# FFN matmuls on x * (1 + scale), with the RMS factor and the shift applied to their result

## The chip, the cores and the metric

One NeuronCore of a Trainium2 chip runs the whole program. The metric is the device time of one execution, in microseconds: the median of several runs.

## The reference, cut to what matters

The program is one inference step of a small diffusion backbone with 128 context tokens and 512 latent tokens of 1024 channels. Four layers have the mixers Fourier, pooling, latent attention and Fourier again; each mixer is followed by a gated ConvFFN (2816 gate and 2816 value channels). Context and latent tokens have shifts, scales and gates of their own, and are separate sequences for the convolution.

```
def modulate(x, shift, scale):
    return rms_norm(x) * (1 + scale) + shift          # rms_norm: x * rsqrt(mean(x*x) + eps), per token
def dwconv3(u, w, b):                                   # zeros beside the first and the last token
    up = jnp.pad(u, ((0, 0), (1, 1), (0, 0)))
    return up[:, :-2] * w[0] + up[:, 1:-1] * w[1] + up[:, 2:] * w[2] + b
def conv_ffn(h, w_in, w_conv, b_conv, w_out):
    u = dwconv3(h @ w_in, w_conv, b_conv)
    gate, val = jnp.split(u, 2, axis=-1)
    return (jax.nn.silu(gate) * val) @ w_out
...
    sh1, sc1, g1, sh2, sc2, g2 = split(silu(cond) @ w_ada[i] + b_ada[i], 6)
    x = x + g1 * mixer(modulate(x, sh1, sc1))
    x = x + g2 * conv_ffn(modulate(x, sh2, sc2), w_ffn_in[i], ...)
```

## The kernel before

Activations lie with channels on the 128 partitions: `x` is 8 chunks of 128 channels by W = 644 token columns, context in columns 0 to 127, latent in 130 to 641, gaps between and behind. A matrix product is made of three fp32r products: every operand is split into a rounded part (`_hi`) and the remainder (`_lo`), and hi*hi, hi*lo and lo*hi are summed. One result (128 output channels by all tokens) takes 8 chunks x 3 products x 2 halves of 322 columns = 48 matmuls into one of two PSUM accumulators, `acc[0]` and `acc[1]`, in turn. TensorE (PE) may start result j + 2 only when result j has been taken out of its accumulator (`result_taken`).

The weights come as one stream of units of 512 KB, in a fixed order (`_stream`), through four slots `raw`: SyncE (SP) loads the next unit of a slot once the slot's last unit is done (`unit_done`). A weight unit is rounded by ScalarE (ACT, L790) as soon as the result two places ahead is ready, and its remainder is taken by GpSimd (POOL, L344), which frees the slot. A modulation unit is 128 rows of `w_ada`: VectorE (DVE) multiplies it by the two conditions, with a running sum (`modulate`, L1261, two products of 128x1024), which frees its slot. The 48 modulation units of the next layer are computed in this layer's FFN.

A mixer ends in a projection of eight results. DVE adds each, times its gate, to a chunk of `x` (`update_x`, L1239, three pieces), ACT squares the chunk (L840), and DVE adds the squares (L1248). In layer 0 the projection also computes eight modulation units, in steps of `PRODUCT_STEPS`. In the pooling layer a projection result takes only 12 matmuls.

The FFN begins with `norm`: PE sums the squares over channels with a matmul by ones (`statistics`, L462), ACT takes the root (L804), DVE the reciprocal (L1154); then for every chunk DVE scales (L1163) and modulates (L1185), ACT rounds (L832), POOL takes the remainder (L354). PE's `first_two` takes the chunks of the first two results as they come.

FFN-in and FFN-out go in three parts of 8, 8 and 6 pairs (`PARTS`). A pair is a gate result and a value result. For each, ACT rounds the next weight, then writes the centre tap and bias (L887, L893), and DVE adds the left and right taps (L1307, L1311), which frees the accumulator. ACT takes the silu of the gate (L890), DVE multiplies by the value (L1317), ACT rounds (L896), DVE takes the remainder (L1321). In the layers before the last, DVE computes one modulation unit ahead of each pair and one after the gate's taps. A part ends in eight FFN-out results of 8, 8 or 6 chunks, each added to `x`; part 1 has four more modulation units there.

Of the kernel before, what the change touches and what calls it, by code (L numbers as in the profile page):

```python
# [28 lines left out]
GAP = 2  # L29
LAT0 = CTX + GAP  # L30
LAT1 = LAT0 + LAT
W = LAT1 + GAP
# [16 lines left out]
KW = KEYS + GAP  # L49
# [22 lines left out]
Q_TILES = [(LAT0 + P * t, LAT0, SHALF, 2) for t in range(4)] + [(0, 0, CTX, 1)]  # L72
# [11 lines left out]
def ada_in_ffn(layer):  # L84

    return layer + 1 < DEPTH

ADA_EXTRA, EXTRA_PART = MODS - 2 * PAIRS, 1  # L90

FIRST_MODS, PRODUCT_MODS = 2 * KC, KC
# [17 lines left out]
def extra(layer, part):  # L112
    return ADA_EXTRA if ada_in_ffn(layer) and part == EXTRA_PART else 0


class Counts:


    def __init__(self):
        self.unit = 0  # L120
        self.result = 0
        self.split = 0
        self.ada = 0
        self.pair = 0
        self.rounded = 0
        self.stat = 0
        self.chunk = 0
        self.full = 0
        self.affine = 0
        self.squared = 0  # L130
        self.score = 0
        self.cleared = 0
# [8 lines left out]
def build_backbone(nc, a):  # L141
# [8 lines left out]
    with ExitStack() as ctx:  # L150
# [30 lines left out]
        gate_pool = place("gate_pool", [P, KC, 2])  # L181
        top, negtop, total, inverse = (place(n, [P, 2]) for n in ("top", "negtop", "total", "inverse"))
# [43 lines left out]
        sum_q, rstd_q = row(3), row(4)  # L226
        probs = [row(3), row(4)]
# [37 lines left out]
        h_ready = sem("h_ready")  # L265
        mod_ready = sem("mod_ready")
# [23 lines left out]
        CXS, LTS = slice(0, CTX), slice(LAT0, LAT1)  # L290
# [21 lines left out]
        def after_ffn_in(n, layer, count):  # L312
            n.unit += 4 * count if ada_in_ffn(layer) else 2 * count
            n.split += 2 * count
            n.result += 2 * count
            n.pair += count
            n.ada += 2 * count if ada_in_ffn(layer) else 0

        def after_project(n, units=KC, squares=True):
            n.unit += units  # L320
            n.split += units
            n.result += KC
            n.squared += KC if squares else 0
# [15 lines left out]
        def _(pool):  # L339
# [43 lines left out]
            def project(size, last=False):  # L383

                for j in range(6 if last else 8):
                    ring((j + 2) % SLOTS, n.split + 2 + j, size if j < 6 else UNIT)

            def ffn(layer):
                lo_parts()
                n.stat += 1  # L390
                for part, (_, count) in enumerate(PARTS):
                    if ada_in_ffn(layer):
                        with pool.Fori(0, count) as i:
                            ring(0, n.split + 2 * i + 2)
                            ring(1, n.split + 2 * i + 3)
                    else:
                        with pool.Fori(0, count // 2) as i:
                            for j in range(4):
                                ring((j + 2) % SLOTS, n.split + 4 * i + 2 + j)
                    after_ffn_in(n, layer, count)  # L400
                    project(count * P, part == 2 and layer == DEPTH - 1)
                    after_project(n, squares=part == 2)
# [33 lines left out]
        def _(pe):  # L436
# [80 lines left out]
            def ffn(layer):  # L517
                norm()
                for part, (_, count) in enumerate(PARTS):
                    turn = 1 if ada_in_ffn(layer) else 2  # L520

                    def gate_or_value(i, j):
                        pe.wait_ge(unit_done[j], n.unit // SLOTS + i + 1)
                        pe.wait_ge(result_taken, n.result + 2 * turn * i + j - 1)
                        for k in range(KC):
                            done = product(acc_halves(j % 2), weights(j, k),
                                           token_halves(h_hi[:, k, :], h_lo[:, k, :]), k == 0, k == KC - 1)
                        done.then_inc(result_ready, 1)

                    if part == 0:  # L530

                        first_two()
                        for j in range(2, 2 * turn):
                            gate_or_value(0, j)
                    with pe.Fori(int(part == 0), count // turn) as i:
                        for j in range(2 * turn):
                            gate_or_value(i, j)
                    after_ffn_in(n, layer, count)
                    project((g_hi, g_lo), count, g_ready, n.pair - count, (extra(layer, part), 0))
                    after_project(n, squares=part == 2)  # L540

            def fnet(layer):
                r = n.result
                for g in range(GROUPS):
                    for t in range(5):

                        first = 0 if t == 0 else LAT0 + P * (t - 1)
# [95 lines left out]
            def attention():  # L643
                with pe.Fori(0, 2) as i:
                    for h2 in range(2):
# [22 lines left out]
                        def values(t):  # L668

                            p = accumulator(V_RESULT + t)  # L670
                            first = [0, LAT0, LAT0 + P, LAT0 + 2 * P, LAT0 + 3 * P, LAT1][t]
# [111 lines left out]
        def _(act):  # L783
# [24 lines left out]
            def norm(layer, shift, scale, mine=lambda c: False, target=None, after_root=None, after_chunk=None):  # L808
# [4 lines left out]
                for c in range(KC):  # L813
                    out = row(HF + c % 2) if target is None else padded[c % 2]
                    if mine(c):
                        act.wait_ge(xn_ready, n.chunk + c + 1)
# [20 lines left out]
                n.chunk += KC  # L837

# [3 lines left out]
            def project_steps(i, squares, rounds=4):  # L842

                for j in range(4):
                    if j < rounds:
                        round_ring((j + 2) % SLOTS, n.unit // SLOTS + i + (j + 2) // SLOTS + 1, n.result + 4 * i + j + 1)
                    if squares:
# [921 lines left out]
```

## Time and profile before

| what | us |
|---|---|
| median of 3 runs | 3133.83 |
| lowest and highest run | 3130.42, 3135.1 |
| span of the profiled execution, first to last instruction | 3126.8 |
| median less that span | 7.0 |
| PE busy / DVE busy / POOL busy in the span | 2755.8 / 1636.7 / 946.0 |

The busy times are sums over the span, and engines work side by side, so they don't add up to it. The profile gives no time of its own for the profiled execution beside its span; the runs are timed separately.

### The profile page before, as it was taken

The page shows a single profiled execution, that of the slowest core. Times are in us where ns is not written, and L with a number is a line of the kernel's source. Part 1 is how long each engine was busy: PE and PEld are TensorE (multiplying, and loading weights), DVE is VectorE, ACT ScalarE, POOL GpSimd, SP SyncE. Part 2 cuts the span into 40 slices and gives each one's busy share as a digit, 9 for nine tenths or more (in the row PEclk, how much of TensorE's full clock was granted, in tenths as well). Part 3 has the DMA queues.
Part 4 walks back from the last instruction along what each step waited for, and adds up shares of the span by engine and source line. Part 5 has one row for each costly group of instructions (what it writes and reads, how often), then busy time and mean ns, then how long its engine had stood idle before and what let it go on. Part 6 is the DMA issues. An engine that isn't in the chain of part 4 may idle for free.

```text
span 3126.8 us, 46036 instructions
## 1 busy us (share of the span) xinstructions
PE 2755.8 (88%) x17344; PEld 2663.9 (85%) x17344; DVE 1636.7 (52%) x2448; ACT 919.5 (29%) x1247; POOL 946.0 (30%) x420
## 2 busy tenths in 40 slices
PE   3887999997399999978898987999999697999997
PEld 3676999996299999977887886999999487999997
DVE  7667636465875574654433335736655525323235
ACT  3112323233232232332322223323223322323232
POOL 2014333333543333332110113333333213333332
PEclk9998999998699999989988888999999898999999
DMA  7332424343033343321110111424433101222221
GB/s 254 101 121 95 145 92 144 127 138 105 27 115 121 114 149 113 132 71 65 41 41 28 36 46 40 154 101 135 146 116 121 62 21 50 72 74 74 74 74 68
DMA packets 83942, 297.48 MB, mean 95 GB/s; under 512 B 10048, under 2 KB 11520, under 8 KB 83456
## 3 DMA queue, kind: packets, MB, share of 16 engines
q1 hardware_dynamic: 78336, 285.25, 27.2%
q10 hardware_dynamic: 5504, 10.79, 1.0%
q8 instruction: 74, 1.21, 0.2%
q14 instruction: 28, 0.23, 0.0%
HBM read 293.07 MB, written 2.93 MB: 95 GB/s over the span
## 4 chain that ended last, share of the span: by engine, by line
PE 78%; DVE 13%; ACT 3%; issue 3%; DMA 1%; POOL 1%; ACTq 0%; DVEq 0%; SPq 0%; POOLq 0%
PE acc L443 75%; DVE rows L1185 2%; DVE rows L1163 2%; PE sacc L443 2%; DVE rows L1154 1%; DMA raw<-in_stream 1%; DVE products L1261 1%; DVE rows L1248 1%; DVE pt_lo L1206 1%; PE sacc L462 1%; PE acc L700 1%; POOL w_lo L344 0%; DVE scratch L1405 0%; DVE x L1239 0%; POOL h_lo L354 0%
## 5 line engine op out<-in xcount | busy, mean ns | idle before, releaser
L344 POOL TENSOR_TENSOR w_lo<-raw,w_hi 128x1024 fp32r<-128x1024 f32 (+2 forms) x336 | 815.7, 2428 | 2021.1 <-ACT w_hi L790 2021.1
L443 PE MATMUL acc<-h_hi,w_hi 128*128 128x322 f32 x3408 | 802.9, 317 | 152.4 <-POOL h_lo L354 76.1
L443 PE MATMUL acc<-h_lo,w_hi 128*128 128x322 f32 x3408 | 798.1, 316 | 0.0
L443 PE MATMUL acc<-h_hi,w_lo 128*128 128x322 f32 x3408 | 792.1, 314 | 0.0
L443 PEld LDWEIGHTS acc<-h_hi,w_hi 128*128 128x128 f32 x3408 | 583.6, 192 | 171.4 <-issue 113.3
L790 ACT ACTIVATE w_hi<-raw 128x1024 fp32r<-128x1024 f32 (+2 forms) x336 | 350.2, 1043 | 1060.6 <-PE acc L443 1008.3
L443 PEld LDWEIGHTS acc<-h_lo,w_hi 128*128 128x128 f32 x3408 | 587.9, 193 | 0.0
L443 PEld LDWEIGHTS acc<-h_hi,w_lo 128*128 128x128 f32 x3408 | 587.8, 193 | 0.0
L1261 DVE SCALAR_TENSOR_TENSOR products<-raw,cond 128x1024 f32<-128x1024 f32 x372 | 474.2, 1315 | 18.3 <-ACT cond L1101 8.6
L1239 DVE SCALAR_TENSOR_TENSOR x<-acc,mod,x 128x128 f32 (+1 forms) x360 | 136.4, 434 | 453.3 <-PE acc L443 453.3
L1307 DVE SCALAR_TENSOR_TENSOR conv<-acc,conv_w,conv 128x644 f32<-128x644 f32 x176 | 156.6, 890 | 399.3 <-ACT conv L893 292.7
L443 PE MATMUL acc<-g_hi,w_hi 128*128 128x322 f32 x1408 | 328.1, 314 | 18.7 <-DVE g_lo L1321 13.2
L443 PE MATMUL acc<-g_lo,w_hi 128*128 128x322 f32 x1408 | 326.9, 313 | 0.0
L443 PE MATMUL acc<-g_hi,w_lo 128*128 128x322 f32 x1408 | 326.6, 313 | 0.0
L443 PEld LDWEIGHTS acc<-g_hi,w_hi 128*128 128x128 f32 x1408 | 241.3, 191 | 22.7 <-DVE g_lo L1321 16.5
L443 PEld LDWEIGHTS acc<-g_lo,w_hi 128*128 128x128 f32 x1408 | 240.9, 191 | 0.0
L443 PEld LDWEIGHTS acc<-g_hi,w_lo 128*128 128x128 f32 x1408 | 240.6, 190 | 0.0
L1248 DVE TENSOR_TENSOR rows<-rows 128x644 f32<-128x644 f32 x82 | 122.3, 1491 | 120.7 <-ACT rows L840 62.1
L1311 DVE SCALAR_TENSOR_TENSOR conv<-acc,conv_w,conv 128x644 f32<-128x644 f32 x176 | 156.6, 890 | 27.7 <-DVE conv L1307 27.0
L896 ACT ACTIVATE g_hi<-gated 128x644 f32 x88 | 65.4, 743 | 273.3 <-DVE gated L1317 273.3
L890 ACT ACTIVATE gated<-conv 128x644 f32<-128x644 f32 x88 | 65.8, 748 | 190.1 <-DVE conv L1311 190.1
L1321 DVE TENSOR_TENSOR g_lo<-gated,g_hi 128x644 f32 x88 | 73.1, 831 | 91.5 <-ACT g_hi L896 91.5
(155 smaller groups left out, 2540.7 us busy)
## 6 DMA issues: line engine op xcount, KB each, us to landing
raw<-in_stream SPq DMA_DIRECT2D x544, 512.0 KB, 3.3
x<-in_x ACTq DMA_DIRECT2D x8, 322.0 KB, 10.2
out_y<-y ACTq DMA_DIRECT2D x8, 322.0 KB, 3.0
cond<-in_cond ACTq DMA_DIRECT2D x2, 1024.0 KB, 6.3
inv_count<-in_inv_count ACTq DMA_DIRECT2D x1, 1328.0 KB, 6.3
rows<-in_rope ACTq DMA_DIRECT2D x1, 644.0 KB, 4.7
conv_w<-in_conv_w ACTq DMA_DIRECT2D x4, 88.0 KB, 2.0
cache<-in_cache ACTq DMA_DIRECT2D x1, 320.0 KB, 2.9
```

Source lines behind the costliest of these rows:

```text
L344: nc.gpsimd.tensor_tensor(lo, raw[slot][:, 0:raw_size], hi.bitcast(f32), ALU.subtract).then_inc(unit_done[slot], 1)
L443: done = nc.tensor.matmul(o, lhs[lp], r, start=first and z == 0, stop=last and z == 2)
L790: nc.scalar.activation(hi, raw[slot][:, 0:size], ACT.Copy).then_inc(weights_hi, 1)
L890: nc.scalar.activation(gated[:], conv[0][:, 1:W + 1], ACT.Silu).then_inc(silu_done, 1)
L896: nc.scalar.activation(g_hi[:, ds(gate, 1), :].rearrange("p o t -> p (o t)"), gated[:], ACT.Copy).then_inc(g_rounded, 1)
L1163: nc.vector.tensor_tensor(row(XN[c % 3]), x[:, c, :], row(RSTD), ALU.mult).then_inc(xn_ready, 1)
L1239: done = nc.vector.scalar_tensor_tensor(xs, acc[pair][:, bank, p0:p0 + x1 - x0], gate(cond_), xs, ALU.mult, ALU.add)
L1248: nc.vector.tensor_tensor(total_, total_, row(SQ), ALU.add).then_inc(inc, 1)
L1261: nc.vector.scalar_tensor_tensor(out[z][:], raw[slot][:], 1.0, cond[:, z, :], ALU.mult, ALU.mult, accum_out=mod[:, layer % 2, ds(index, 1) ...
L1307: nc.vector.scalar_tensor_tensor(to, halves(acc[half]), tap(0), to, ALU.mult, ALU.add).then_inc(left_done, 1)
L1311: nc.vector.scalar_tensor_tensor(to, halves(acc[half]), tap(2), to, ALU.mult, ALU.add).then_inc(result_taken, 1)
L1321: nc.vector.tensor_tensor(g_lo[:, gc, :].rearrange("p o t -> p (o t)"), gated[:], g_hi[:, gc, :].rearrange("p o t -> p (o t)").bitcast(f32 ...
```

## The change

RMSNorm's factor is one number per token, so it commutes with the product over channels. The FFN now multiplies `x * (1 + scale)`, split into `g_hi` and `g_lo` chunk by chunk in the mixer's projection (`scaled_hi` on ACT, `scaled_lo` on DVE). The shift, negated, is put into the gap columns, so that the product with the weights comes out there too (`gaps_hi`, `gaps_lo`): columns 0 and 643 and the two between the sequences. `x` starts at column 1, and the latent tokens at 131.

Each FFN-in result is then multiplied in PSUM, by DVE, by the tokens' RMS factor (`token_rstd`, 1 in the gaps). With minus the shift's product beside the first and last token, and the shift's product times the sum of the three taps added afterwards (`minus_taps`, `shift_out`), the convolution's zero padding comes out as in the reference. That sum and the convolution's bias go into the silu's bias for the gate, and into the multiplication for the value, which is now two instructions (context and latent).

PE's statistics stand within the first FFN result, after chunk 3 (`STATS_AFTER`). Root and reciprocal follow, and the first rescale waits for them. POOL takes no remainders of the FFN's input any more. The results of a part go through `h_hi` and `h_lo` instead of `g_hi` and `g_lo`.

The modulation units: one per pair, after the gate's rescale and ahead of its taps, and 13 in the FFN-out of parts 0 and 1 each (`ADA_AFTER_OUT`). The FFN's loops over pairs and results are written out.

```
+ADA_AFTER_OUT = (2, 2, 2, 2, 2, 1, 1, 1)
...
+def ada_after(layer, kind, part, i):
+    if layer + 1 == DEPTH:
+        return 0
+    if kind == "in":
+        return 1 - i % 2
+    return ADA_AFTER_OUT[i] if part < 2 else 0
...
+def ffn_stream(layer):
+    weights = ffn_weights()
+    order, at, ada_at = [], [], []
+    for n, w in enumerate(weights):
+        at.append(len(order))
+        order.append(w)
+        for _ in range(ada_after(layer, *weights[n - 2]) if n >= 2 else 0):
+            ada_at.append(len(order))
+            order.append(("ada", 0, len(ada_at) - 1))
+    return order, at + [len(order), len(order) + 1], ada_at
...
# PE, ffn
+                    if kind == "in":
+                        if j == 0:
+                            pe.wait_ge(gaps_ready, layer + 1)
                         for k in range(KC):
+                            if j == 0:
+                                pe.wait_ge(h_ready, n.chunk - KC + k + 1)
                             done = product(acc_halves(j % 2), weights(j, k),
+                                           token_halves(g_hi[:, k, :], g_lo[:, k, :]), k == 0, k == KC - 1)
+                            if j == 0 and k == STATS_AFTER:
+                                pe.wait_ge(summed, n.squared)
+                                statistics(row(SUM))
...
# ACT, a mixer's projection
+            def scaled_hi(layer, c):
+                chunk = lambda t, cols: t[:, ds(c, 1), cols].rearrange("p o t -> p (o t)")
+                for z, cols in enumerate((CXS, LTS)):
+                    done = nc.scalar.activation(chunk(g_hi, cols), chunk(x, cols), ACT.Copy,
+                                                scale=mod[:, layer % 2, ds(SC2 + c, 1), z:z + 1
+                                                          ].rearrange("p o t -> p (o t)"))
+                done.then_inc(h_rounded, 1)
...
# ACT, ffn
+                    if kind == "in":
+                        pair, half = i // 2, i % 2
+                        act.wait_ge(rescaled, 2 * (n.pair + pair) + half + 1)
+                        nc.scalar.activation(two(conv[half][:, 1:W + 1]), halves(acc[half]), ACT.Copy,
+                                             scale=conv_w[:, pair + half * PAIRS, 1:2]).then_inc(centered, 1)
+                        if half == 0:
+                            act.wait_ge(result_taken, n.result + j + 1)
+                            for z, cols in enumerate((CXS, LTS)):
+                                done = nc.scalar.activation(gated[:, cols], conv[0][:, cols.start + 1:cols.stop + 1],
+                                                            ACT.Silu, bias=shift_out[:, 0, z:z + 1])
+                            done.then_inc(silu_done, 1)
...
# DVE, a mixer's projection
+            def scaled_lo(layer, c):
+                dve.wait_ge(h_rounded, n.chunk + c + 1)
+                part = lambda t, cols: t[:, ds(c, 1), cols].rearrange("p o t -> p (o t)")
+                for z, cols in enumerate((CXS, LTS)):
+                    done = nc.vector.scalar_tensor_tensor(part(g_lo, cols), part(x, cols), mod_gate(layer, SC2)(c)(z),
+                                                          part(g_hi, cols).bitcast(f32), ALU.mult, ALU.subtract)
+                done.then_inc(h_ready, 1)
...
# DVE, ffn
-                norm(layer, SH2, SC2)
+                dve.wait_ge(rooted, n.stat + 1)
+                for cols in (CXS, LTS):
+                    done = nc.vector.reciprocal(token_rstd[:, cols], row(RSTD)[:, cols])
...
+                    if kind == "out":
...
+                        dve.wait_ge(result_ready, n.result + j + 1)
+                        update_acc(i, mod_gate(layer, G2)(i), j % 2)
+                        if part == 2:
+                            sum_square(n.squared + i)
+                        units(after)
+                        continue
...
+                    dve.wait_ge(result_ready, n.result + j + 1)
+                    nc.vector.tensor_tensor(halves(acc[half]), halves(acc[half]), two(token_rstd), ALU.mult
+                                            ).then_inc(rescaled, 1)
+                    units(after)
+                    dve.wait_ge(centered, k + 1)
+                    nc.vector.tensor_scalar(shift_out[:, half, :], acc[half][:, 0, C1:LAT0],
+                                            minus_taps[:, channel:channel + 1], tap(3), ALU.mult, ALU.add)
+                    to = two(conv[half][:, 2:W + 2])
+                    nc.vector.scalar_tensor_tensor(to, halves(acc[half]), tap(0), to, ALU.mult, ALU.add
+                                                   ).then_inc(left_done, 1)
+                    dve.wait_ge(left_done, k + 1)
+                    to = two(conv[half][:, 0:W])
+                    nc.vector.scalar_tensor_tensor(to, halves(acc[half]), tap(2), to, ALU.mult, ALU.add
+                                                   ).then_inc(result_taken, 1)
+                    if half == 0:
+                        continue
...
+                    for z, cols in enumerate((CXS, LTS)):
+                        done = nc.vector.scalar_tensor_tensor(
+                            gated[:, cols], conv[1][:, cols.start + 1:cols.stop + 1], shift_out[:, 1, z:z + 1],
+                            gated[:, cols], ALU.add, ALU.mult)
+                    done.then_inc(gated_done, 1)
```

## Rows read from the trace of the kernel before

**Rows 1.** The page's busy times, share of the span and instructions of each engine.
```profile
PE 2755.8 (88%) x17344; PEld 2663.9 (85%) x17344; DVE 1636.7 (52%) x2448; ACT 919.5 (29%) x1247; POOL 946.0 (30%) x420
```

**Rows 2.** Busy time by stretch: us and count by engine, granted clock, DMA.
```profile
184.00:250.44 66.44, 60.42 (x384) 59.62 (x384) 46.28 (x71) 12.41 (x14) 18.18 (x7) 0.95 0.34 115
250.44:287.78 37.34, 17.20 (x64) 14.42 (x65) 31.57 (x39) 9.67 (x12) 16.03 (x9) 0.68 0.17 64
288.00:393.70 105.70, 105.70 (x710) 105.70 (x710) 73.95 (x106) 38.71 (x46) 39.80 (x15) 1.00 0.42 144
841.21:876.10 34.89, 15.39 (x65) 12.36 (x65) 29.93 (x38) 8.82 (x12) 16.03 (x9) 0.71 0.05 16
1912.31:1956.22 43.91, 21.74 (x100) 18.30 (x101) 33.23 (x41) 14.85 (x17) 17.46 (x10) 0.73 0.06 16
2604.48:2639.37 34.89, 15.61 (x64) 12.56 (x64) 26.87 (x34) 9.79 (x12) 15.06 (x9) 0.71 0.05 15
```

**Rows 3.** Chain of waits, layer 3, mixer's end to FFN: start us, us, what.
```profile
2599.99 4.49 PE acc L443 x30
...
2606.01 0.75 ACT rows L840
...
2606.79 1.89 DVE rows L1248
...
2608.72 2.53 PE sacc L462 x4
...
2612.16 4.19 DVE rows L1154
```

**Rows 4.** Timeline of one gate result in FFN-in: start us, us, engine, instruction.
```profile
633.67 1.06 ACT L790 ACTIVATE w_hi<-raw 128x1024 fp32r<-128x1024 f32 x1 [6.11 <-PE acc L443]
634.64 0.88 ACT L887 ACTIVATE conv<-acc,conv_w 128x644 f32<-128x644 f32 x1
...
634.81 2.40 POOL L344 TENSOR_TENSOR w_lo<-raw,w_hi 128x1024 fp32r<-128x1024 f32 x1 [3.78 <-ACT w_hi L790]
...
635.67 0.89 DVE L1307 SCALAR_TENSOR_TENSOR conv<-acc,conv_w,conv 128x644 f32<-128x644 f32 x1 [3.54 <-ACT conv L887]
636.72 0.89 DVE L1311 SCALAR_TENSOR_TENSOR conv<-acc,conv_w,conv 128x644 f32<-128x644 f32 x1 [0.16 <-DVE conv L1307]
```

**Rows 5.** Timeline where a unit meets POOL; spread of the unit's line (min/median/max ns).
```profile
627.56 1.22 DVE L1261 SCALAR_TENSOR_TENSOR products<-raw,cond 128x1024 f32<-128x1024 f32 x1
...
628.70 3.42 DVE L1261 SCALAR_TENSOR_TENSOR products<-raw,cond 128x1024 f32<-128x1024 f32 x1
...
627.64 3.39 POOL L344 TENSOR_TENSOR w_lo<-raw,w_hi 128x1024 fp32r<-128x1024 f32 x1 [4.78 <-ACT w_hi L790]
...
L1261 DVE SCALAR_TENSOR_TENSOR products<-raw,cond x372: 1211/1221/3435, 14.2 to 2373.4; 128x1024 f32<-128x1024 f32 x186
```

**Rows 6.** Groups by line (busy us, mean ns), and one line's spread (min/median/max ns).
```profile
L1321 DVE TENSOR_TENSOR g_lo<-gated,g_hi 128x644 f32 x88 | 73.1, 831 | 91.5 <-ACT g_hi L896 91.5
...
L1278 DVE TENSOR_SCALAR mod<-mod 128x16 f32<-128x16 f32 x8 | 1.1, 172 | 0.2
...
L823 ACT ACTIVATE rows<-rows,mod x16: 477/647/802, 59.7 to 2453.5; 128x128 f32<-128x128 f32 x8, 128x512 f32<-128x512 f32 x8
```

**Rows 7.** Timeline of ACT in layer 0's projection: a weight that came late.
```profile
229.49 1.06 ACT L790 ACTIVATE w_hi<-raw 128x1024 fp32r<-128x1024 f32 x1 [12.41 <-DMA raw<-in_stream]
```

**Rows 8.** Timeline of DVE in the pool layer: first and last residual update.
```profile
820.99 1.13 DVE L1239 SCALAR_TENSOR_TENSOR x<-acc,gate_pool,x 128x128 f32<-128x128 f32 x3
...
841.21 1.13 DVE L1239 SCALAR_TENSOR_TENSOR x<-acc,gate_pool,x 128x128 f32<-128x128 f32 x3
```

**Rows 9.** Waits of PE in layer 0's FFN: us in total, times, longest.
```profile
PE acc L443 <- DVE g_lo L1321: 3.3, 3, 2.3
PE acc L443 <- POOL w_lo L344: 1.8, 1, 1.8
```

**Rows 10.** Timeline of PE in the attention: a wait without a cause in the trace.
```profile
1668.08 1.00 PE L443 MATMUL acc<-ckv_hi,w_hi 128*128 128x386 f32 x2 [3.54 <-issue]
```

More of the change, by code:

```diff
@@ L70 @@
 V_RESULT = 4
-Q_TILES = [(LAT0 + P * t, LAT0, SHALF, 2) for t in range(4)] + [(0, 0, CTX, 1)]
+Q_TILES = [(LAT0 + P * t, LAT0, SHALF, 2) for t in range(4)] + [(C0, C0, CTX, 1)]
 FIRST_LOADS = 16 * 3
@@ L309, in head_out, with after_project @@
             return dst[:, ds(4 * i + 2 * h2 + hh, 1), q0:q0 + P].rearrange("p o t -> p (o t)")
[L312 to L319, printed above, removed]
+        def after_project(n, units=KC):
             n.unit += units
@@ L322, in after_project, with after_ffn @@
             n.result += KC
-            n.squared += KC if squares else 0
+            n.squared += KC
+        def after_ffn(n, layer):
+            order, at, ada_at = ffn_stream(layer)
+            n.unit += len(order)
+            n.split += len(at) - 2
+            n.result += len(at) - 2
+            n.pair += PAIRS
+            n.ada += len(ada_at)
+            n.squared += KC
         @block.sync
@@ L517, in ffn @@
             def ffn(layer):
[L518 to L524, printed above, removed]
+                n.chunk += KC
+                _, at, _ = ffn_stream(layer)
+                for j, (kind, part, i) in enumerate(ffn_weights()):
+                    unit = n.unit + at[j]
+                    first, count = PARTS[part]
+                    pe.wait_ge(unit_done[unit % SLOTS], unit // SLOTS + 1)
+                    pe.wait_ge(result_taken, n.result + j - 1)
+                    if kind == "in":
+                        if j == 0:
+                            pe.wait_ge(gaps_ready, layer + 1)
@@ L535, in ffn @@
[L535 to L540, printed above, removed]
+                                           token_halves(g_hi[:, k, :], g_lo[:, k, :]), k == 0, k == KC - 1)
+                            if j == 0 and k == STATS_AFTER:
+                                pe.wait_ge(summed, n.squared)
+                                statistics(row(SUM))
+                    else:
+                        for k in range(count):
+                            if i == 0:
+                                pe.wait_ge(g_ready, n.pair + first + k + 1)
+                            done = product(acc_halves(j % 2), weights(j, k),
+                                           token_halves(h_hi[:, k, :], h_lo[:, k, :]), k == 0, k == count - 1)
@@ L542, in fnet @@
+                    done.then_inc(result_ready, 1)
+                after_ffn(n, layer)
             def fnet(layer):
@@ L906, in fnet @@
+                after_ffn(n, layer)
             def fnet(layer):
@@ L961, in pool_mix @@
                     square(x[:, j, :])
+                    scaled_hi(layer, j)
+                n.chunk += KC
                 after_project(n, 4)
@@ L1224, in unit @@
                     n.ada += 1
-                for _ in range(before):
-                    unit()
+                gaps_lo(layer)
                 for j in range(KC):
-                    update_x(j, j, gate(j), j % 2, squares)
+                    update_x(j, j, gate(j), j % 2, True)
+                    scaled_lo(layer, j)
                     for _ in range(steps[j]):
```

310 lines of the change are left out of this document (156 added, 154 removed).

## The prediction

> **What bounds the kernel now.** The page comes first: TensorE (PE) is busy for 88% of the span, VectorE (DVE) for about half, and GpSimd (POOL) for a third [rows 1]. Then the busy time by stretch, to see where PE is not busy [rows 2]. In the FFN stretch it runs 710 matmuls in 105.7 us, 0.149 us each, with no gap: 48 matmuls, one result, take 7.16 us, and the gate and value results of a pair 14.3 us. There the hardware loops cost nothing, and neither do the modulation units (two per pair, four products on DVE). The four other stretches of [rows 2] run from the end of the mixer's last result to the moment when PE is steady again in the FFN (in the pool layer from the start of the last residual update). In 37.34, 34.89, 43.91 and 34.89 us, PE does 60, 60, 96 and 60 matmuls beside the 4 of the statistics. Less 0.149 us for each, 28.4, 26.0, 29.6 and 26.0 us are lost, 110 us together. The chain of waits shows by what, for layer 3 [rows 3]: update, square (0.75), adding the square (1.89), the statistics (2.53 on PE), root, reciprocal (4.19), and after that scaling, modulation, rounding and remainder chunk by chunk until 2639.37. The granted clock of these stretches is 0.68 to 0.73 [rows 2], between the levels of 1.2 and 2.4 GHz; the loss includes that.
>
> **What the change takes away.** The FFN input no longer waits for the norm. Chunks 0 to 3 of the first result can run as soon as the mixer's last result is out (call it E): 24 x 0.149 = 3.6 us. Then the statistics, which start at E + 4.24 and end at E + 6.77 as now [rows 3]; the remainder of chunk 7 is ready by then (square's sum at E + 4.2, plus two subtractions of about 1.0 us together, by the 0.831 of [rows 6]). Chunks 4 to 7 follow. So 6.77 - 3.6 = 3.2 us are lost instead of 26 to 30.
>
> The root and reciprocal now run beside chunks 4 to 7. Root to E + 7.6, the reciprocal of 640 columns 4.2 [rows 3], fills, tap sums, then the first rescale at about E + 13.2, while result 0 is ready at E + 10.4. It has until E + 17.5, when result 1 is ready and PE wants the buffer back. With rescale, one unit and two taps it is free at about E + 18.6: 1.1 us late, some 0.25 us over the stall below, for three layers 0.75 us.
>
> **What it adds in the mixers.** Per chunk, two ScalarE (ACT) multiplications by (1 + scale) and two DVE remainders. The nearest ACT row has two pointer operands, 0.48 to 0.80 us [rows 6]; a plain rounding would be less, so 0.9 to 1.28 us, 1.1 taken. In the projections of layers 2 and 3 this hides behind 7.16 us of PE per result. In the pool layer nothing hides it, since a chunk there is a serial chain: update, square, sum. Seven chunks take 841.21 - 820.99 = 20.2 us [rows 8], 2.89 each. With the new work update 1.13, square 0.7, ACT 1.1, remainder 1.0 and handovers give 4.1: 8.5 us more, and 2.0 lost after the last update. In layer 0 the projection already loses 66.44 - 57.2 = 9.2 us [rows 2], because its units and weights share four slots and ACT waits for a weight [rows 7]. DVE gets 1 us more per result, of which I carry 2.0 us to the end, plus 0.4 before the statistics. The starts then cost 5.6 + 10.5 + 3.2 + 3.2 + 0.75 = 23 us, and the gain is 110 - 23 = **87 us**.
>
> **What it adds in the FFN.** Now the gate result of a pair, from its readiness T [rows 4]: ACT rounds the next weight, POOL starts its 2.40 us subtraction at T + 1.19, ACT scales the centre, and DVE adds the taps (0.89 + 0.15 + 0.89); PE gets the buffer at T + 4.1 and needs it at T + 7.16. A unit comes after this. In the new order DVE first rescales in PSUM, then computes a unit, then the taps. No row has DVE writing PSUM: between 0.83 (the SBUF remainder, [rows 6]) and twice 0.89; 0.89 taken, and either is covered by POOL's turn.
>
> The unit is the point. A product alone takes 1.21 us, but its longest is 3.435 [rows 5]. At 627.56 a product starts, POOL 0.08 us behind it; POOL takes 3.39 instead of 2.40, and the second product, due at 628.70, ends at 632.12, 1.09 after POOL. They don't run together, and POOL gets the next turn; the taps, which read PSUM, keep their 0.89 beside it [rows 4]. In the new order the unit meets POOL's subtraction in every pair. If POOL is first, it ends at T + 3.58 and the products at T + 5.82; if the first product is first, POOL ends at T + 4.4 and the unit at T + 5.5. DVE is done with the preceding pair only some 0.5 us after T (the silu, the second rounding and the value half are pushed back with the taps), so POOL is first. Then the shift's bias (0.17 to 0.27 us, by the 16-column row of [rows 6] and a pointer more), and taps of 1.93: PE restarts at T + 8.0, **0.85 us late**. Bounds: 0 if unit and POOL did not collide, 0.5 if the product is first, 1.2 if each small step costs 0.1 more. The value half has time to spare. 22 pairs in 3 layers: 66 x 0.85 = **56 us**. Layer 3 has no units, and its gate buffer is free by T + 4.4.
>
> The Trainium skill, "SBUF — State Buffer", section "SBUF: two separate sides", says that a DVE operation with two SBUF inputs and a GpSimd one lock the shared ports for a whole instruction. The trace agrees (3.42 us for 1.22); by it the rescale, with one input in PSUM, and the taps go free. By the rule the FFN stalls as I take it, without it not at all.
>
> From FFN-in to FFN-out the last remainder of a part now lags the stalls: PE idles 1.6, 1.6 and 3.4 us at the three parts, against 3.3 + 1.8 now [rows 9] (the 1.8, a weight behind four units, goes). That is 1.5 a layer in three layers and 0.25 per part in layer 3: **5 us**.
>
> The units moved to FFN-out: five results of eight in two parts get two. POOL again goes first, so DVE ends them at T + 8.1, 1 us into the next result, where the update fits beside POOL. PE needs only the update, done at T + 2.1. Slots: the next units' loads can start at T + 3.6 and T + 5.8, the next weight's at T + 8.1; with 3.5 us each the weight lands near T + 11.6 and is rounded at T + 14.3. Cost nothing, with 2.7 us of cover. Unrolled loops: nothing. One wait at the head of a long loop's second pass shows 3.54 us without a cause [rows 10]; straight-line stretches before it show none.
>
> **Sum**, on the profiled span of 3126.8: -87 + 56 + 5 = -26, hence 3101. The median of the runs, 3133.8, lies 7.0 above that span, which I carry: **3108 us**.
>
> **Rivals.**
> A, unit and POOL do not collide (the unit gets through before POOL, or ACT's rounding is late). For it: 1.221 is the median product [rows 5]. Against: POOL starts 1.14 after ACT in [rows 4]. Then the 56 goes: 3133.8 - 87 + 5 = 3052.
> B, slower: the four slots stall PE in FFN-out. For it: three loads of 512 KB per result, and layer 0's projection loses 9.2 us over eight results with eight units. Against: there the weights stand ahead of the units, here they alternate, with 2.7 us to spare. At 9.2 us in each of six stages 55 us: 3163. It decides from 26 / 6 = 4.3 us a stage.
> C, the starts are shortened less: the first rescale waits for root, reciprocal, fills and taps. Each us beyond E + 13.2 costs one us in each layer; at 6 us the gain is gone: 3132.
>
> **How the numbers follow.** Forecast 0.60, A 0.17, B 0.10, C 0.13. The forecast's own range, by 0.5 to 1.1 us of stall, is 3085 to 3125. The range, 3054 to 3136, takes in A's end and C's, and leaves B and the tails out. 0.2% is 6 us, about what the runs' spread of 4.7 us can tell. Faster: nearly all of the forecast (0.57), A, and 0.06 of C: 0.80. The same: 0.03 and 0.05: 0.08. Slower: B and 0.02: 0.12.
>
> **What would show it.** Right: at the four starts a PE gap of 1 us before the statistics, no lowered clock, h_lo of POOL gone. In the FFN of layers 0 to 2 a pair of 15.1 us, the second product at 3.4 or the first delayed; in layer 3 14.3. Pairs of 14.3 everywhere show A; PE waiting for w_lo in FFN-out shows B; a first rescale later than E + 14 shows C. I am wrong if a stall stands where I have none, above all in layer 3.

## The result, and the profile after

The changed kernel takes 3059.5 us (median of 4 runs, 3056.5 to 3062.1) against 3132.1 us of the kernel before on the same chip (4 runs, 3129.3 to 3135.1): ratio 0.9773, 95% interval 0.9758 to 0.9789, or 73 us less. I had forecast 3108. The direction and the range held; the change is nearly three times the 26 us of my sum. The profiled execution took 3058.1 us with a span of 3056.2, so the two profiled spans differ by 70.6 us.

The page's busy times, the line that answers to [rows 1]: DVE is busy 337 us longer, POOL 40 us less. Not all of the 337 is work: a product that waits for POOL counts as busy, and the same 372 products take 189 us more (their row on the page before, L1261, and on the page after, L1330). The new rescales are 147 us.

```profile
PE 2737.8 (90%) x17344; PEld 2641.5 (86%) x17344; DVE 1973.7 (65%) x2900; ACT 919.0 (30%) x1375; POOL 905.9 (30%) x388
...
L1261 DVE SCALAR_TENSOR_TENSOR products<-raw,cond 128x1024 f32<-128x1024 f32 x372 | 474.2, 1315 | 18.3 <-ACT cond L1101 8.6
L1330 DVE SCALAR_TENSOR_TENSOR products<-raw,cond 128x1024 f32<-128x1024 f32 x372 | 663.3, 1828 | 9.3 <-ACT cond L1143 8.1
```

Busy time by stretch (columns as in [rows 2]): the four starts, from the mixer's last result (pool layer: from the start of the last residual update) to steady work of PE, and 105.7 us of layer 0's FFN.

```profile
252.34:273.04 20.70, 17.14 (x101) 16.32 (x100) 17.62 (x34) 8.07 (x12) 4.74 (x2) 0.92 0.47 161
836.24:853.76 17.52, 14.78 (x84) 13.84 (x83) 14.68 (x30) 5.70 (x8) 4.74 (x2) 0.90 0.23 72
1878.41:1897.12 18.71, 15.61 (x100) 14.78 (x100) 15.82 (x30) 9.85 (x11) 4.91 (x2) 1.00 0.21 67
2557.40:2574.70 17.30, 15.60 (x100) 14.77 (x100) 13.52 (x26) 6.76 (x9) 4.80 (x2) 1.00 0.18 62
288.00:393.70 105.70, 103.17 (x684) 101.50 (x684) 83.40 (x111) 36.04 (x49) 38.53 (x15) 1.00 0.34 107
```

When PE is steady, two whole results (96 matmuls, 14.3 us) are done. So the starts lose 6.4, 3.2, 4.4 and 3.0 us. Layer 0's last projection result comes 1.9 us later than before (252.34 for 250.44), and the pool layer's chunk takes 3.81 us instead of 2.89, 6.4 us over seven. With these the losses are 8.3, 9.6, 4.4 and 3.0 us, 25 together, where 110 were lost before. The 1.9 us are not shown to come from the change: in three profiles of each kernel (experiment 8), layer 0's statistics start at 256.1, 259.4 and 257.7 us before, and at 258.7, 258.3 and 257.9 after. The granted clock of the last two starts is 1.00, for 0.73 and 0.71 in [rows 2]. The last line shows the price: 684 matmuls where the same length held 710 before (0.96 us of it is a wait at the end of part 0, which falls into this window only after the change).

The chain of waits at layer 3's start (start us, us, what), against [rows 3]: the statistics take 1.37 us instead of 2.53, and root, reciprocal and fills run while PE has the other chunks. PE waits for the first pair's taps until 2574.70, and from there on runs 672 matmuls in 100.11 us, 0.149 each, without a gap: layer 3 has no units and no stall.

```profile
2561.71 1.37 PE sacc L491 x4
...
2563.93 4.17 DVE rows L1353 x2
...
2568.92 1.47 DVE minus_taps L1365
...
2570.85 0.85 DVE acc L1399
...
2574.70 100.11 PE acc L472 x672
```

The timeline of one pair in layer 0's FFN-in, to be read against [rows 4, 5]; the gate result is ready at about T = 280.42, when its last two matmuls (from 279.94) are through.

```profile
279.54 0.83 DVE L1423 TENSOR_TENSOR h_lo<-gated,h_hi 128x644 fp32r<-128x644 f32 x1 [0.81 <-ACT h_hi L936]
280.24 0.46 PE L472 MATMUL acc<-g_hi,w_hi 128*128 128x322 f32 x2
280.44 0.84 DVE L1399 TENSOR_TENSOR acc<-acc,rows 128x644 f32<-128x644 f32 x1
280.50 1.06 ACT L822 ACTIVATE w_hi<-raw 128x1024 fp32r<-128x1024 f32 x1 [0.99 <-PE acc L472]
281.19 1.22 DVE L1330 SCALAR_TENSOR_TENSOR products<-raw,cond 128x1024 f32<-128x1024 f32 x1
281.64 3.01 POOL L377 TENSOR_TENSOR w_lo<-raw,w_hi 128x1024 fp32r<-128x1024 f32 x1 [4.27 <-ACT w_hi L822]
282.33 3.40 DVE L1330 SCALAR_TENSOR_TENSOR products<-raw,cond 128x1024 f32<-128x1024 f32 x1
...
286.77 0.89 DVE L1410 SCALAR_TENSOR_TENSOR conv<-acc,conv_w,conv 128x644 f32<-128x644 f32 x1
287.57 0.83 DVE L1399 TENSOR_TENSOR acc<-acc,rows 128x644 f32<-128x644 f32 x1
287.80 0.53 PE L472 MATMUL acc<-g_hi,w_hi 128*128 128x322 f32 x2 [0.27 <-DVE conv L1410]
...
295.21 0.84 DVE L1399 TENSOR_TENSOR acc<-acc,rows 128x644 f32<-128x644 f32 x1
```

The unit does meet POOL: its second product takes 3.40 us and POOL 3.01. But DVE is done with the preceding pair at 280.37, 0.05 us ahead of T, so the first product starts 0.45 us ahead of POOL. The taps end at T + 7.24. PE began the value result at 280.24, could begin the next gate result 7.16 us later, at 287.40, and begins it at 287.80. The next rescale of a gate comes 14.77 us after the last (280.44 to 295.21), 0.47 over the 14.30 of a pair of layer 3, which has no stall (seven pairs in the 100.11 us above).

PE's waits in layer 2's FFN (us in total, times, longest), against [rows 9]: taps and remainders, no weight.

```profile
PE acc L472 <- DVE conv L1410: 7.2, 19, 2.4
PE acc L472 <- DVE h_lo L1423: 4.3, 3, 2.4
```

### The profile page after: what moved, and what is told of

It reads as the page before. It is cut to its first block, busy times and chain, and to the rows that moved or that the text cites. A ratio compares the mean times of both kernels' runs of the same rounds, so it can differ in the third digit from the quotient of the medians.

```text
span 3056.2 us, 43498 instructions
## 1 busy us (share of the span) xinstructions
PE 2737.8 (90%) x17344; PEld 2641.5 (86%) x17344; DVE 1973.7 (65%) x2900; ACT 919.0 (30%) x1375; POOL 905.9 (30%) x388
## 4 chain that ended last, share of the span: by engine, by line
PE 64%; DVE 26%; issue 5%; ACT 4%; DMA 1%; POOL 0%; ACTq 0%; DVEq 0%; SPq 0%; POOLq 0%
PE acc L472 61%; DVE products L1330 11%; DVE conv L1410 2%; DVE conv L1406 2%; PE sacc L472 2%; DVE rows L1317 1%; DVE rows L1205 1%; DVE rows L1196 1%; DVE rows L1227 1%; DVE x L1311 1%; DVE pt_lo L1249 1%; DVE shift_out L1403 1%; DVE rows L1353 1%; ACT w_hi L822 1%; DMA raw<-in_stream 1%
## 5 line engine op out<-in xcount | busy, mean ns | idle before, releaser
L472 PE MATMUL acc<-g_hi,w_hi 128*128 128x322 f32 x2816 | 654.8, 313 | 21.1 <-DVE conv L1410 19.4
L1330 DVE SCALAR_TENSOR_TENSOR products<-raw,cond 128x1024 f32<-128x1024 f32 x372 | 663.3, 1828 | 9.3 <-ACT cond L1143 8.1
L472 PE MATMUL acc<-g_lo,w_hi 128*128 128x322 f32 x2816 | 650.7, 312 | 0.0
L472 PE MATMUL acc<-g_hi,w_lo 128*128 128x322 f32 x2816 | 649.5, 311 | 0.0
L472 PE MATMUL acc<-h_hi,w_hi 128*128 128x322 f32 x2000 | 475.5, 320 | 109.0 <-POOL h_lo L399 51.2
L472 PEld LDWEIGHTS acc<-g_hi,w_lo 128*128 128x128 f32 x2816 | 479.0, 189 | 0.0
L472 PE MATMUL acc<-h_lo,w_hi 128*128 128x322 f32 x2000 | 470.7, 317 | 0.0
L472 PE MATMUL acc<-h_hi,w_lo 128*128 128x322 f32 x2000 | 468.0, 316 | 0.0
L472 PEld LDWEIGHTS acc<-h_hi,w_hi 128*128 128x128 f32 x2000 | 345.4, 194 | 122.4 <-issue 73.8
L472 PEld LDWEIGHTS acc<-h_lo,w_hi 128*128 128x128 f32 x2000 | 347.9, 194 | 0.0
L472 PEld LDWEIGHTS acc<-h_hi,w_lo 128*128 128x128 f32 x2000 | 347.5, 194 | 0.0
```

The lines of the kernel that those rows point to most:

```text
L472: done = nc.tensor.matmul(o, lhs[lp], r, start=first and z == 0, stop=last and z == 2)
L1330: nc.vector.scalar_tensor_tensor(out[z][:], raw[slot][:], 1.0, cond[:, z, :], ALU.mult, ALU.mult, accum_out=mod[:, layer % 2, ds(index, 1) ...
```

## The experiments

Four questions were open: how the unit and POOL stall a pair, whether the order of the two decides the size, what the statistics' speed hangs on, and why layer 2's attention, which the change leaves alone, was 11 us shorter in the profile after. Experiment 4 takes the change apart, 6 and 7 go on from it. In the diffs, minus lines are those of the changed kernel.

**1. The unit behind the taps.**

```
                     nc.vector.tensor_tensor(halves(acc[half]), ...).then_inc(rescaled, 1)
-                    units(after)
                     dve.wait_ge(centered, k + 1)
...
                     ... tap(2) ... .then_inc(result_taken, 1)
+                    units(after)
                     if half == 0:
                         continue
```

> The gate half's unit stands behind the two taps instead of ahead of them. Theory (turns): the 0.45 us that a pair of layers 0 to 2 loses (14.77 against 14.32 in layer 3's pace) is the unit's second product waiting out POOL's subtraction with the taps queued behind it. Then the pair falls to 14.3 and 66 pairs give back about 30 us: 3030 us, with the products at 1.2 us each, since POOL is done by T + 4. Rival (chain): the rescale, the shift's bias and the scaled centre are by themselves too long for the buffer. Then the pair stays near 14.8 and the time at 3059 us.

Measured: 3025.4 us, ratio 0.9667 (0.9644 to 0.9689), 33 us below the changed kernel by the two ratios. DVE's timeline: rescale, products undisturbed, and the next gate's rescale 14.27 us later. PE's waits for remainders fall too, to 3.0 us a layer from 4.4. The rival falls.

```profile
293.61 0.84 DVE L1399 TENSOR_TENSOR acc<-acc,rows 128x644 f32<-128x644 f32 x1 [0.54 <-PE acc L472]
...
297.37 1.22 DVE L1330 SCALAR_TENSOR_TENSOR products<-raw,cond 128x1024 f32<-128x1024 f32 x1
298.51 1.22 DVE L1330 SCALAR_TENSOR_TENSOR products<-raw,cond 128x1024 f32<-128x1024 f32 x1
...
307.88 0.84 DVE L1399 TENSOR_TENSOR acc<-acc,rows 128x644 f32<-128x644 f32 x1 [0.54 <-PE acc L472]
```

**2. The unit where it was, POOL later.** ACT rounds the next weight behind the scaled centre in the gate half.

```
-                    if j + 2 < len(weights) or layer < DEPTH - 1:
-                        round_unit(...)
+                    if not gate and (j + 2 < len(weights) or layer < DEPTH - 1):
+                        ahead()                       # the same round_unit
...
                         nc.scalar.activation(two(conv[half][:, 1:W + 1]), ...).then_inc(centered, 1)
+                        if gate:
+                            ahead()
```

> DVE's order stays; only ACT's rounding of the next weight stands behind the scaled centre in the gate half, so that POOL's subtraction starts some 1.3 us later, at about T + 2.9. Theory (turns): both products run before POOL, the taps end near T + 5.4, and the pair falls to 14.3: 3030 us. Rival (work): it is the unit's 2.4 us of work ahead of the taps that stalls, whatever POOL does: the pair stays at 14.8, 3059 us.

Measured: 3018.8 us, ratio 0.9645 (0.9615 to 0.9675), 40 us below the changed kernel by the ratios; from the first experiment it can't be told. With the unit still ahead of the taps, both products run in 1.22 us, POOL comes just before the second ends, and the pair takes 14.27.

```profile
295.56 0.84 DVE L1405 TENSOR_TENSOR acc<-acc,rows 128x644 f32<-128x644 f32 x1 [0.54 <-PE acc L472]
296.31 1.22 DVE L1336 SCALAR_TENSOR_TENSOR products<-raw,cond 128x1024 f32<-128x1024 f32 x1
297.45 1.22 DVE L1336 SCALAR_TENSOR_TENSOR products<-raw,cond 128x1024 f32<-128x1024 f32 x1
298.26 2.68 POOL L377 TENSOR_TENSOR w_lo<-raw,w_hi 128x1024 fp32r<-128x1024 f32 x1 [6.23 <-ACT w_hi L822]
...
309.83 0.84 DVE L1405 TENSOR_TENSOR acc<-acc,rows 128x644 f32<-128x644 f32 x1 [0.54 <-PE acc L472]
```

So the stall is the meeting, not the unit's work. The Trainium skill, "SBUF — State Buffer", section "SBUF: two separate sides", says that of a DVE operation with two SBUF inputs and a GpSimd one that reads SBUF the one that starts first keeps the shared ports for its whole length; the 3.40 of the changed kernel and the 1.22 here agree with it.

**3. POOL first.** Three operations of two columns, their result unused, delay the unit behind POOL.

```
+                    for d in range(3 * after):
+                        nc.vector.tensor_scalar(spare[:, d, :], minus_taps[:, 0:2], minus_taps[:, 2:3], tap(3),
+                                                ALU.mult, ALU.add)
                     units(after)
```

> Three small DVE operations (about 0.5 us together, their result unused) stand between the gate half's rescale and its unit, so that POOL's subtraction starts ahead of the first product. Theory (turns, the order decides): the unit then ends 0.77 us later than now however long the small operations take between 0.45 and 1.2 us, and the pair goes from 14.77 to about 15.5: +50 us, 3110 us, with a first product of about 3.2 us and two undisturbed ends. Rival (the order does not matter): the pair grows by the small operations alone, 0.5 us: +33 us, 3093.

Measured: 3108.5 us, ratio 0.9919 (0.9893 to 0.9944), 46 us above the changed kernel. The pair takes 15.36 us. One detail was not as expected: the small operations themselves wait out POOL (2.88 us for three that take 0.66 at 276.13, where POOL is idle), and the products behind them run free.

```profile
276.13 0.66 DVE L1403 TENSOR_SCALAR spare<-minus_taps,conv_w 128x2 f32<-128x2 f32 x3
...
289.85 0.46 PE L473 MATMUL acc<-g_hi,w_hi 128*128 128x322 f32 x2
...
290.05 0.83 DVE L1400 TENSOR_TENSOR acc<-acc,rows 128x644 f32<-128x644 f32 x1 [1.59 <-PE acc L473]
290.79 2.88 DVE L1403 TENSOR_SCALAR spare<-minus_taps,conv_w 128x2 f32<-128x2 f32 x3
291.24 2.40 POOL L378 TENSOR_TENSOR w_lo<-raw,w_hi 128x1024 fp32r<-128x1024 f32 x1 [5.82 <-ACT w_hi L823]
293.58 1.21 DVE L1331 SCALAR_TENSOR_TENSOR products<-raw,cond 128x1024 f32<-128x1024 f32 x1
...
298.01 0.54 PE L473 MATMUL acc<-g_hi,w_hi 128*128 128x322 f32 x2 [0.88 <-DVE conv L1414]
...
305.41 0.84 DVE L1400 TENSOR_TENSOR acc<-acc,rows 128x644 f32<-128x644 f32 x1
```

The unit ends at 295.95, 5.9 us after the rescale began, against 5.3 in the changed kernel. The stall is 15.36 - 14.30 = 1.06 us; for POOL first I had forecast 0.85. The value result begins at 289.85, 0.18 us before T as above, so T is 290.03 and PE goes on at T + 7.98 (298.01), where the prediction has T + 8.0; but it could have begun at 289.85 + 7.16, which is T + 6.98 and not T + 7.16. The growth of 0.59 is between the 0.5 and the 0.77 of the two expectations, and the small operations were longer than I took them (0.66 undisturbed, for 0.5), so the size alone decides nothing. The timeline does: POOL takes its turn first, the small operation that stands there waits for its end, and the products behind it no longer stretch.

**4. The units as before, with the new algebra.** Two per pair and four in part 1's FFN-out: the one half of the change alone.

```
     if kind == "in":
-        return 1 - i % 2
-    return ADA_AFTER_OUT[i] if part < 2 else 0
+        return 1
+    return int(part == 1 and i < 4)
```

> The new FFN with the units placed as before: two per pair in FFN-in and four in FFN-out of part 1. Theory (turns): a unit that meets POOL takes 4.5 us of DVE; two of them with two rescales (1.7), two biases (0.5), four taps (3.5), gating (0.75) and remainder (0.8) come to 16.4 us, so DVE becomes the bound of a pair: about 2 us over 14.77, 66 times, 130 us: 3190 us. Rival (only the gate half's buffer is short): one more stall of 0.45 per pair, 3090 us. If the moving of the units did nothing, 3059.

Measured: 3082.7 us, ratio 0.9846 (0.9822 to 0.987), 23 us above the changed kernel: neither number came. POOL does not hold up the second unit, because in the value half ACT rounds the weight behind the silu, and POOL comes when the second product already runs. There it is POOL that waits (3.20 us for 2.40):

```profile
291.39 1.22 DVE L1330 SCALAR_TENSOR_TENSOR products<-raw,cond 128x1024 f32<-128x1024 f32 x1
292.53 1.22 DVE L1330 SCALAR_TENSOR_TENSOR products<-raw,cond 128x1024 f32<-128x1024 f32 x1
292.81 3.20 POOL L377 TENSOR_TENSOR w_lo<-raw,w_hi 128x1024 fp32r<-128x1024 f32 x1 [5.08 <-ACT w_hi L822]
```

DVE then fills the pair (14.86 us, 283.52 to 298.38) and falls behind, so PE waits longer for the last remainder of each part: 7.5 us in layer 0 instead of 4.4. By the ratios the change is worth 71 us: the new algebra with the units as before gives 48 of them (0.9846), and the moving of the units the other 23. Of these 23, PE's waits for taps and remainders in the whole profile show 15 (50.3 us against 35.5); where the others lie is not shown.

**5. The statistics ahead of chunk 0.**

```
+                            if j == 0 and k == 0:
+                                pe.wait_ge(summed, n.squared)
+                                statistics(row(SUM))
                             done = product(...)
-                            if j == 0 and k == STATS_AFTER:
-                                ...
```

> The changed kernel with the statistics ahead of chunk 0 of the first FFN result instead of behind chunk 3, so that PE stands idle for about 4.2 us before them, as it did before. Theory (the statistics took 1.37 us instead of 2.53 because PE was at work until just before them): they take 2.5 us again, and each of the four starts loses 4.2 + 2.5 - 3.6 hidden, less what the wait for the rescale hides: between 1.2 and 5 us a layer, 5 to 20 in all, 3065 to 3080 us. Rival (it is the other code around them): they stay at 1.4 us.

Measured: 3067.9 us, ratio 0.9806 (0.9782 to 0.9829), 10 us above the changed kernel, with intervals that overlap. PE waits 4.3 us for the sum in layer 3, as it did before the change, and the statistics of the four starts take 2.48 to 2.49 us. The chain of layer 2:

```profile
1885.75 2.49 PE sacc L491 x4
```

The windows of the statistics (columns as in [rows 2]) have the clock, here in layer 2 and in the changed kernel in layer 3:

```profile
1885.75:1888.24 2.49, 2.49 (x5) 1.69 (x6) 0.78 (x2) 0.15 (x1) 0.00 (x0) 0.50 0.67 211
2561.71:2563.08 1.37, 1.37 (x6) 1.04 (x7) 0.87 (x2) 0.00 (x0) 0.00 (x0) 1.00 0.59 176
```

So the statistics run in 1.37 us where PE was at work until 0.7 us before (layers 2 and 3, granted clock 1.00, the level of 2.4 GHz), and in 2.49, near twice as long, after 4.3 us of rest or more (granted clock 0.50, the level of 1.2 GHz). Between these it is not fixed: in layer 0 of the changed kernel PE rests 2.75, 3.14 and 3.28 us before them in its three profiles, and they take 1.35, 2.52 and 1.83 us. The rival falls: all four starts went back to 2.5 us, and in layer 0 one and the same code gives three durations.

**6. Shorter head.** The first edit, and the fills and tap sums ahead of the wait for the root.

```
-                dve.wait_ge(rooted, n.stat + 1)
-                for cols in (CXS, LTS): ... reciprocal ...
                 for cols in (slice(0, C0), slice(C1, LAT0), slice(LAT1, W)): ...
                 ... minus_taps ...
+                dve.wait_ge(rooted, n.stat + 1)
+                for cols in (CXS, LTS): ... reciprocal ...
+                clear_sum()
```

> The gate half's unit behind the taps, as in the first experiment, and besides the fills and the two tap sums of the FFN's head ahead of the wait for the root. Theory (the first rescale still comes late in every layer, by the work between reciprocal and rescale): the first rescale comes 1 to 2 us earlier, the 0.8 to 0.95 us that PE waits for the first pair's taps go, and the four layers give back 3 to 5 us: about 3021 us beside 3025. Rival (hidden: PE has the second result to work on meanwhile): no change that can be measured, 3025 us.

Measured: 3013.4 us, ratio 0.9635 (0.961 to 0.9659). The wait is gone from the chain: behind layer 3's statistics PE runs on for 124 matmuls and more.

```profile
2511.34 1.35 PE sacc L491 x4
2512.69 18.42 PE acc L472 x124
```

In time it can't be told from the first edit alone (0.9644 to 0.9689). Its median is the lowest of all versions, 117 us below the kernel before on its chip; the interval of the second experiment overlaps with its own as well.

**7. The way from FFN-in to FFN-out.** The first two results of each part, interleaved on PE, on top of the sixth edit.

```
+                        if i == 0:
+                            pe.wait_ge(unit_done[unit % SLOTS], unit // SLOTS + 1)     # the second result's weight
+                            pe.wait_ge(result_taken, n.result + j)
+                            for k in range(count - 1):
+                                out(j + 1, k)
+                            pe.wait_ge(g_ready, n.pair + first + count)
+                            out(j, count - 1).then_inc(result_ready, 1)
+                            done = out(j + 1, count - 1)
```

> The kernel with early fills, and besides the first two FFN-out results of each part interleaved on PE: all pairs but the last for both, then the last pair's for both. Theory (PE waits at the three transitions of a layer only for the last pair's remainder, 3.0 us per layer with the units out of the way, 4.4 in the changed kernel): the waits go, and the four layers give back 12 us: about 3001 us beside 3013. Rival (the wait moves to the second result's weight or buffer): the waits stay, under another name, 3013 us.

Measured: 3055.5 us, ratio 0.9775 (0.9753 to 0.9796), 42 us slower than the sixth. PE's waits in layer 0's FFN:

```profile
PE acc L472 <- POOL w_lo L377: 9.9, 3, 3.9
```

The remainder's wait is gone, and a worse one stands in its place. By the edit both weight buffers come free at almost the same moment, and the chain at the first transition shows the third result's weight behind it: PE until 383.32, rounding 1.07, POOL 3.28, PE from 388.07. The rival's place was right; its price, none, was not. In the four layers these waits are 35.6 us, where the sixth had 12.0 for remainders, 24 more. Of the other 18 us the two profiles show 13 in layer 2's attention (558.5 and 545.2 us from statistics to statistics), a stretch that differs between executions of one kernel too, as the next experiment shows.

**8. The same kernels again.** For the stretch of layer 2's attention.

> The kernel before once more, unchanged, for the stretch from the start of layer 2's norm statistics to the start of its FFN statistics: 561.8 us in the profile before, 551.0 after, with the same code. Theory (the change sets the pace there, by when the stretch begins): 561.8 again within 2 us. Rival (it differs from execution to execution): another value, anywhere from 548 to 562.

> The changed kernel once more, unchanged, for the same stretch of layer 2. Theory (the change sets the pace there): 551.0 us again within 2 us. Rival (it differs from execution to execution): another value from 548 to 562.

> A third profile of the kernel before, for the stretch of layer 2 from the last chunk of the attention's norm to the FFN's statistics: 531.2 and 525.3 us in the two so far. If the pace there differs from execution to execution and the code around it does not matter, it falls anywhere between 515 and 531; if the kernel before is slower there, between 525 and 531.

> A third profile of the changed kernel, for the same stretch: 520.4 and 528.8 us in the two so far. If the pace differs from execution to execution alone, it falls anywhere between 515 and 531; if the changed kernel is faster there, nearer to 520 than the kernel before.

The first two expectations count from the norm's statistics, the others from the chunk behind that norm with which PE begins; I use the latter, up to the FFN's statistics. The stretch ends with the projection, where the change does add work on ACT and DVE, and after the change it holds the first 24 matmuls of the FFN besides. Counted from the norm's statistics, the three profiles have 561.8, 555.9 and 557.9 us before, and 551.0, 559.4 and 551.0 after: the first theory (the same again within 2 us) fails for both kernels. From the chunk on, the kernel before gives 531.2, 525.3 and 527.3 us, the changed one 520.4, 528.8 and 520.4. Windows of that stretch (columns as in [rows 2]), the second profile of the kernel before:

```profile
1385.92:1911.19 525.27, 462.65 (x2897) 436.57 (x2897) 205.85 (x405) 155.76 (x322) 91.04 (x44) 0.91 0.14 48
```

The first profile of the changed kernel, and then its second:

```profile
1362.35:1882.71 520.36, 459.54 (x2920) 434.32 (x2920) 212.01 (x422) 164.44 (x341) 91.09 (x44) 0.92 0.15 48
```

```profile
1365.86:1894.63 528.77, 469.75 (x2921) 444.33 (x2921) 212.46 (x422) 164.92 (x341) 91.14 (x44) 0.90 0.14 47
```

One and the same kernel differs by 8.4 us, with the same matmuls, and the granted clock moves with it (0.92 and 0.90). So the 10.9 us between the first two profiles are not shown to come from the change. The means, 527.9 and 523.2, differ by 4.7 us, less than that; whether the change has a share in it stays open.

## Why the prediction was right or wrong

By the two profiled spans, term by term (us):

| term | predicted | measured |
|---|---|---|
| the four starts | -87 | -85, and -4.5 of small waits right behind them |
| stall of the FFN pairs, layers 0 to 2 | +56 | +28 |
| FFN-in to FFN-out | +5 | -2 |
| layer 2's attention with its projection | 0 | -11 |
| rest | 0 | +4 |
| sum | -26 | -71 |

The stall is 0.47 us for 20 pairs in three layers; the first pair of a layer lies in the start, and the last has none (its next weight is shorter). The rest is mainly layer 3's mixer with its projection: 2.9 us longer from statistics to statistics (185.2 us, and 182.6 and 185.3 in the other two profiles of the changed kernel; 182.3 in each of the kernel before). So of the 45 us by which the sum was off, 28 are the stall and 7 the transitions; the last two rows, 7 us net, lie in stretches that differ by as much between executions of one kernel, and are luck as far as is shown.

**The step that failed** is "DVE is done with the preceding pair only some 0.5 us after T", and from it "so POOL is first". No row stood behind the 0.5. DVE is done 0.05 us before T. I had pushed the silu, the second rounding and the value half back against a fixed T, but T is moved by the same stall. The value result is ready when DVE turns to it (rescale at 287.57, straight behind the gate's tap), and nothing accumulates. With rescale at once, the product starts at T + 0.77 and POOL at T + 1.22: a margin of 0.45 us, and my estimate was 0.55 off. Both ends of the unit were about right: I had T + 5.5 if the product is first and T + 5.82 if POOL is, and the traces show T + 5.3 and, in experiment 3, T + 5.9. I chose the wrong one, and half of the 56 us went with it. The lower bound that I named for this case, 0.5, was nearly the value, but by two errors that mostly cancel: PE goes on at T + 7.4, for the T + 7.66 that 0.5 late meant, and could have done so at T + 7.0, for my T + 7.16. With POOL first the second error stands alone (1.06 us of stall for 0.85).

**The transitions** were mis-sized by 7 us: PE waits 4.4 us per layer for remainders (3.0 in layer 3) in place of 3.3 and 1.8, so the weight that no longer comes late is worth more than the lag.

**The starts** were right as a sum and nearly so one by one: 8.3, 9.6, 4.4 and 3.0 us for my 5.6, 10.5, 3.2 and 3.2 with 0.75 besides. Two errors cancel. The statistics are faster than I took them (1.37 for 2.53), which experiment 5 ties to the chunks in front. Against that PE waits 2.7 us for them in layer 0, where the last update starts 2.3 us after E (at 254.61), behind the sum and the remainder of the chunk before, and the first taps are later than planned in layer 2: a tap sum of 0.24 us took 1.75, beside POOL. The first rescale comes at E + 13.45 in layer 3, for my 13.2, and at E + 14.1 in layer 0, just past the mark of 14 that I had set for rival C; with 25 us for the four starts C falls all the same. The pool layer's chunk costs 3.81, for my 4.1.

**The rivals.** A (no meeting) is refuted for the changed kernel and made true by experiments 1 and 2, which give 33 and 40 us, against 28 for the stall and 4 for the remainders behind it. Its 3052 us is nearer to the 3059.5 than my 3108, but that is a coincidence: the unit and POOL do meet, and without their meeting in FFN-in the time is 3025 (experiment 1). The range that was to take in A's end began at 3054 and left its 3052 out. B is refuted: PE waits for no weight in FFN-out. That layer 3 has no stall held (672 matmuls in 100.11 us). The same row is all there is on the written-out loops: there they show no cost.

**The carry.** The 7.0 us by which the median stood above the span were mostly that execution's luck: for the changed kernel the same execution has 3058.1 for a span of 3056.2.

## What to carry to other kernels

Where two engines take turns at a resource, the sum needs the order first, and an order that hangs on half a microsecond is two cases with a price each, not one. In a loop whose pace the stall itself sets, do not push later steps back against the old clock: let the whole loop slip, and see what is still late. A place where an engine's other work cost nothing here is behind the instruction that frees the accumulator (experiment 1); ahead of it, it cost nothing either once the other engine came later (experiment 2).

## What the runs showed of the hardware

- DVE's rescale reads and writes PSUM and takes 0.84 us for 644 columns, hardly more than the subtraction in SBUF (0.83), and it is not stretched beside POOL (0.84 at 266.45, with POOL at work from 266.35 to 268.74).
- Even a DVE operation of two columns in SBUF waits for POOL's whole subtraction: up to 2.50 us instead of 0.28 (experiment 3).
- Of two products in a row the first does not keep POOL out for the second: POOL, 0.45 us behind the start of the first, gets the next turn, and the second product takes 3.40 us instead of 1.22.
- The same code, layer 2's attention with its projection, ran 520.4 and 528.8 us in two executions of one kernel, at a granted clock of 0.92 and 0.90. A difference of two profiles in such a stretch needs a second profile of each before it is explained.
